# Nine homes for the V blocks, half of their loads begun by ScalarE, gates in groups of eight

## What is computed

```python
q = (xt @ w_q).reshape(T, PEER_HEADS, 2, PEER_DK_HALF)          # T = 512, D = 1024
s1, i1 = lax.top_k(s[:, :, 0], 16); s2, i2 = lax.top_k(s[:, :, 1], 16)
top_s, pos = lax.top_k(cand, 16)                                # 8 heads x 16 experts of 16384
gates = jax.nn.softmax(top_s, axis=-1)
a = jax.nn.gelu(jnp.einsum('cd,ced->ce', xc, u_table[ic]), approximate=False) * gc
out = jnp.einsum('ce,ced->cd', a, v_table[ic])
```

## Time and profile before

| | |
|---|---|
| median of 3 runs | 1637.96 us (1637.13 to 1638.74) |
| profiled execution, own time | 1638.74 us |
| its span | 1636.9 us, so 1.84 us lie around the span |
| TensorE | busy 1593.2 us, 97% |
| VectorE | busy 1275.3 us, 78% |
| ScalarE, GpSimd | 739.5 us, 929.4 us |
| DMA | 457.79 MB, mean 280 GB/s |
| stage V on TensorE | 1104.1 to 1622.3 us |

### The profile page before, as it was taken

How to read it: one execution, slowest core, us unless ns; L and a number is a source line. 1 busy time by engine, 2 the same in 40 slices (tenths; PEclk the granted TensorE clock), 3 DMA queues, 4 the chain that set the end, 5 groups by cost and what they waited for, 6 DMA issues and landing times.

```text
span 1636.9 us, 25955 instructions
## 1 busy us (share of the span) xinstructions
PE 1593.2 (97%) x9763; PEld 1484.6 (91%) x9763; DVE 1275.3 (78%) x2385; ACT 739.5 (45%) x1278; POOL 929.4 (57%) x558
## 2 busy tenths in 40 slices
PE   9999999999999999999999999997999999999996
PEld 7788777788888999999999999997999999999996
DVE  7876635654532899999999878757988899889894
ACT  5533335644321433346677788732333333333333
POOL 4545322434442898898766668786444555546530
PEclk9999999999999999999999999999999999999998
DMA  8321423365443899999988899999999999999981
GB/s 231 104 78 52 116 78 90 91 195 172 116 129 108 300 361 338 347 336 332 341 324 334 300 344 415 418 392 365 407 404 378 389 405 404 406 404 402 404 324 52
DMA packets 215828, 457.79 MB, mean 280 GB/s; under 512 B 14800, under 2 KB 106320, under 8 KB 214168
## 3 DMA queue, kind: packets, MB, share of 16 engines
q1 hardware_dynamic: 145304, 221.29, 39.8%
q0 software_dynamic: 46080, 167.79, 26.4%
q10 hardware_dynamic: 24320, 67.05, 10.6%
HBM read 401.59 MB, written 54.46 MB: 279 GB/s over the span
## 4 chain that ended last, share of the span: by engine, by line
PE 65%; DMA 14%; DVE 12%; issue 4%; ACT 2%; POOL 1%; SPq 0%; POOLq 0%; DVEq 0%; ACTq 0%
PE bank L294 17%; PE bank L296 17%; PE bank L295 17%; DMA raw<-in_v_tab 9%; PE bank L1999 5%; DMA rows<-in_v_tab,expert 2%; DMA mixbuf<-dense_gates 2%; PE x_rows L294 1%; PE x_rows L296 1%; PE x_rows L295 1%; ACT spl_a L284 1%; DVE rows L1376 1%; PE bank L906 1%; POOL spl_a L288 1%; DVE spl_a L288 1%
## 5 line engine op out<-in xcount | busy, mean ns | idle before, releaser
L288 POOL TENSOR_TENSOR spl_a<-raw,spl_a 128x1024 fp32r<-128x1024 f32 x170 | 411.4, 2422 | 217.8 <-ACT spl_a L284 216.1
L284 ACT ACTIVATE spl_a<-raw 128x1024 fp32r<-128x1024 f32 x294 | 309.8, 1056 | 419.1 <-PE bank L296 237.4
L1367 POOL DMA_INDIRECT rows<-in_v_tab,expert x160 | 252.9, 1580 | 216.8 <-DVE hot L1874 193.4
L294 PE MATMUL bank<-x_dense,spl_a 128*128 128x352 f32 x1024 | 335.7, 328 | 6.3 <-ACT gl L1588 6.0
L296 PE MATMUL bank<-x_dense,spl_a 128*128 128x352 f32 x1024 | 329.3, 322 | 0.0
L295 PE MATMUL bank<-x_dense,spl_a 128*128 128x352 f32 x1024 | 328.8, 321 | 0.0
L294 PE MATMUL bank<-aws,spl_a 128*128 128x352 f32 x768 | 249.6, 325 | 20.2 <-DVE aws L1854 17.9
L295 PE MATMUL bank<-aws,spl_a 128*128 128x352 f32 x768 | 248.2, 323 | 0.0
L296 PE MATMUL bank<-aws,spl_a 128*128 128x352 f32 x768 | 248.1, 323 | 0.0
L1376 DVE SCALAR_TENSOR_TENSOR rows<-rows,x_rows 128x1024 f32<-128x1024 f32 x154 | 186.0, 1211 | 28.1 <-DMA rows<-in_u_rows,expert 27.8
L1874 DVE SCALAR_TENSOR_TENSOR hot<-rows,dot_rows,hot 128x1024 f32<-128x1024 f32 x157 | 197.7, 1278 | 4.5 <-DMA rows<-in_v_tab,expert 4.5
(11 more groups left out here) (362 smaller groups left out, 3070.1 us busy)
## 6 DMA issues: line engine op xcount, KB each, us to landing
raw<-in_u_t SPq DMA_DIRECT2D x128, 512.0 KB, 6.2
raw<-in_v_tab SPq DMA_DIRECT2D x128, 512.0 KB, 9.7
dense_gates<-mixbuf ACTq DMA_DIRECT2D x11, 2048.0 KB, 10.9
raw<-in_w_in SPq DMA_DIRECT2D x42, 512.0 KB, 3.9
gelu_ux<-gl ACTq DMA_DIRECT2D x58, 352.0 KB, 6.2
mixbuf<-gelu_ux SPq DMA_DIRECT2D x19, 704.0 KB, 12.7
late_gates<-dense_gates ACTq DMA_DIRECT2D x4, 2816.0 KB, 37.3
mixbuf<-dense_gates ACTq DMA_DIRECT2D x3, 2816.0 KB, 36.5
```

What stands on the lines that cost most here:

```text
L284: eng.activation(spl(n, 0, slice(0, W)), raw[:, s, :], ACT.Copy).then_inc(hi_done, 1)
L288: eng.tensor_tensor(spl(n, 1, slice(0, W)), raw[:, n % RAW, :], spl(n, 0, slice(0, W)).bitcast(F32), ALU.subtract) \
L294: nc.tensor.matmul(out, w_hi, x_hi, start=first, stop=False)
L1367: pool.indirect_dma_start(out=rows[:, g % ROWS, :], out_offset=None, in_=u_rows[:, :] if g < STEPS else v_rows, in_offset=bass.IndirectOff ...
```

## The change

Four things are done.

1. **Raw homes.** The memory of `late_gates` becomes five more homes for raw V blocks (`raw_more`). V's blocks 7 to 11 go there as soon as stage U is over; from then on nine homes are used in turn, so that a load waits for the lower part of the block nine before and no longer four before. SyncE issues the loads of blocks 12, 14, 16, ... and ScalarE those of 13, 15, 17, ..., each at a step of V two apart.
2. **Gates.** They come in groups of 8 blocks (1408 KB, pieces of 1 KB) into two halves of `mixbuf`. Groups 0 and 1 come in stage U where the halves of group 0 came; group g comes at step 8g - 10 of V, and VectorE needs it at its step 8g - 2. All are issued by ScalarE, on the same queue as its V loads.
3. **Exponentials.** `EXP_AT` becomes 22, 46, 69, 93: the first two stand one step of U later.
4. **The start of V.** VectorE instead of GpSimd makes the lower parts of V's blocks 0 to 3, put between its last dot products, of which 6 and not 9 stand behind the wait for the gates, 4 and not 6 of them with the right operand in SBUF. The additions of the V rows are spread over 120 steps from step 2 on instead of 122 steps from step 0 on. The reading of GELU parts stands two steps later.

Its diff, without the lines that only move semaphores or rename:

```diff
@@ -108,7 +108,9 @@
 AWS = 4
 LAST = 2
 KEPT = 12
-GROUP = 16
+GROUP = 8
+MORE = 5
+FAR = 7
 VECTOR_LO = []
 WARM = 5
 
@@ -204,7 +206,8 @@
         x_space = ExitStack()
         x_dense = sb(x_space, "x_dense", [P, 2, KD, DT], F32R)
         x_space.close()
-        late_gates = sb(outer, "late_gates", [P, GROUP * DT])
+        late_space = sb(outer, "raw_more", [P, 2 * KD * DT])
+        raw_more = late_space[:, 0:MORE * W].rearrange("p (s c) -> p s c", s=MORE)
         tiles = sb(outer, "tiles", [P, 2, KD, P])
         dot_rows = sb(outer, "dot_rows", [P, 2 * KD * (T - DT - P)])
         z_row, g_row, a_row = [dot_rows[:, i * STEPS:(i + 1) * STEPS] for i in range(3)]
@@ -239,7 +245,7 @@
 
         def by_vector(n):
 
-            return n in VECTOR_LO or n >= V0 + LEAD
+            return n in VECTOR_LO or n >= V0
 
         def lo_count(n):
 
@@ -249,27 +255,51 @@
 
             eng.wait_ge(lo_vector if by_vector(n) else lo_done, lo_count(n))
 
+        def raw_home(n):
+
+            if n < V0 + FAR:
+                return n % RAW
+            at = (n - V0 - FAR) % (RAW + MORE)
+            return RAW + at if at < MORE else (V0 + FAR + at - MORE) % RAW
+
+        def raw_block(n):
+
+            s = raw_home(n)
+            return raw[:, s, :] if s < RAW else raw_more[:, s - RAW, :]
+
+        def raw_before(n):
+
+            return max([m for m in range(max(0, n - RAW - MORE), n) if raw_home(m) == raw_home(n)], default=None)
+
+        def block_loaded(n):
+
+            s = raw_home(n)
+            return unit_loaded[s] if s < RAW else more_loaded[s - RAW]
+
         def load_unit(sp, n):
 
-            if n >= RAW:
-                wait_lo(sp, n - RAW)
-            s = n % RAW
+            if raw_before(n) is not None:
+                wait_lo(sp, raw_before(n))
+            elif n >= RAW:
+                sp.wait_ge(unit_used, V0)
             if BR0 <= n < WO0:
                 c = (n - BR0) * P
-                dst = raw[:, s, :].rearrange("p (k c) -> p k c", k=KD)
+                dst = raw_block(n).rearrange("p (k c) -> p k c", k=KD)
                 sp.dma_start(dst[:, 0:4, :], w_a[:, c:c + P].rearrange("(k p) c -> p k c", p=P)) \
-                    .then_inc(unit_loaded[s], 16)
+                    .then_inc(block_loaded(n), 16)
                 sp.dma_start(dst[:, 4:8, :], w_b[:, c:c + P].rearrange("(k p) c -> p k c", p=P)) \
-                    .then_inc(unit_loaded[s], 16)
+                    .then_inc(block_loaded(n), 16)
             elif n < U0:
-                sp.dma_start(raw[:, s, :].rearrange("p (k c) -> p k c", k=KD), unit_source(n)) \
-                    .then_inc(unit_loaded[s], 16)
+                sp.dma_start(raw_block(n).rearrange("p (k c) -> p k c", k=KD), unit_source(n)) \
+                    .then_inc(block_loaded(n), 16)
             else:
-                sp.dma_start(raw[:, s, :], unit_source(n)).then_inc(unit_loaded[s], 16)
-
-        def loads_before(n, s):
-
-            return sum(2 if BR0 <= m < WO0 else 1 for m in range(s, n + 1, RAW))
+                sp.dma_start(raw_block(n), unit_source(n)).then_inc(block_loaded(n), 16)
+
+        def loads_before(n):
+
+            s = raw_home(n)
+            loads = sum(2 if BR0 <= m < WO0 else 1 for m in range(n + 1) if raw_home(m) == s)
+            return loads if s < RAW else loads + 1
 
         def last_step(n):
 
@@ -277,15 +307,14 @@
 
         def split_hi(eng, n):
 
-            s = n % RAW
-            eng.wait_ge(unit_loaded[s], 16 * loads_before(n, s))
+            eng.wait_ge(block_loaded(n), 16 * loads_before(n))
             if spl_before(n) is not None:
                 eng.wait_ge(unit_used, last_step(spl_before(n)) + 1)
-            eng.activation(spl(n, 0, slice(0, W)), raw[:, s, :], ACT.Copy).then_inc(hi_done, 1)
+            eng.activation(spl(n, 0, slice(0, W)), raw_block(n), ACT.Copy).then_inc(hi_done, 1)
 
         def split_lo(eng, n):
             eng.wait_ge(hi_done, n + 1)
-            eng.tensor_tensor(spl(n, 1, slice(0, W)), raw[:, n % RAW, :],
+            eng.tensor_tensor(spl(n, 1, slice(0, W)), raw_block(n),
                               spl(n, 0, slice(0, W)).bitcast(F32), ALU.subtract) \
                 .then_inc(lo_vector if by_vector(n) else lo_done, 1)
 
@@ -1311,9 +1338,9 @@
         first_half.close()
         mixbuf = sb(outer, "mixbuf", [P, 24 * DT])
         stage = mixbuf[:, 0:2 * NC * TB].rearrange("p (s c t) -> p s c t", s=2, c=NC)
-        gates_home = [mixbuf[:, 0:GROUP * DT], late_gates[:, :]]
+        gates_home = [mixbuf[:, i * GROUP * DT:(i + 1) * GROUP * DT] for i in range(2)]
         gl = sb(outer, "gl", [P, 4, DT])
-        gelu_home = [gl] + [mixbuf[:, (GROUP + 4 * i) * DT:(GROUP + 4 * i + 4) * DT].rearrange("p (c t) -> p c t", c=4)
+        gelu_home = [gl] + [mixbuf[:, (2 * GROUP + 4 * i) * DT:(2 * GROUP + 4 * i + 4) * DT].rearrange("p (c t) -> p c t", c=4)
                             for i in range(2)]
         rows = sb(outer, "rows", [P, ROWS, D])
         aws = sb(outer, "aws", [P, 2, AWS, DT], F32R)
@@ -1334,16 +1360,18 @@
         row_used = sem("row_used")
         z_gelu = sem("z_gelu")
 
-        def mix_gates(queue, group, first, count, mixed):
-
-            c = expert_chunk(GROUP * group + first)
+        def mix_gates(queue, group):
+
+            c = expert_chunk(GROUP * group)
             home = gates_home[group % 2].rearrange("p (b c t) -> p b c t", c=GROUP, t=TB)
-            tail = min(count, NC - c)
-            queue.dma_start(home[:, :, first:first + tail, :].rearrange("p b c t -> p b (c t)"),
-                            dense_d[:, :, c * TB:(c + tail) * TB].rearrange("b p x -> p b x")).then_inc(mixed, 16)
-            if tail < count:
-                queue.dma_start(home[:, :, first + tail:first + count, :].rearrange("p b c t -> p b (c t)"),
-                                dense_d[:, :, 0:(count - tail) * TB].rearrange("b p x -> p b x")).then_inc(mixed, 16)
+            tail = min(GROUP, NC - c)
+            queue.dma_start(home[:, :, 0:tail, :].rearrange("p b c t -> p b (c t)"),
+                            dense_d[:, :, c * TB:(c + tail) * TB].rearrange("b p x -> p b x")) \
+                .then_inc(gates_mixed[group % 2], 16)
+            if tail < GROUP:
+                queue.dma_start(home[:, :, tail:GROUP, :].rearrange("p b c t -> p b (c t)"),
+                                dense_d[:, :, 0:(GROUP - tail) * TB].rearrange("b p x -> p b x")) \
+                    .then_inc(gates_mixed[group % 2], 16)
 
         def mix_gelu(queue, part_no):
 
@@ -1434,7 +1462,7 @@
             LATE_STEPS = 15
             LATE_DOTS = 15
             SCORES_AT = [0, 0, 0, 8, 14, 19, 24, 30, 35, 41, 46, 52, 58, 64, 70, 76]
-            EXP_AT = [21, 45, 69, 93]
+            EXP_AT = [22, 46, 69, 93]
             SLOTS_AT = [None, 48, 72, 98]
             GATHER_AT = [4, 4, 4, 5, 6, 7, 7, 8, 9, 9, 10, 11, 11, 12, 13, 14, 14, 15, 17, 17, 18, 19, 20, 21, 22,
                          23, 24, 24, 25, 26, 27, 28, 29, 30, 30, 31, 32, 33, 34, 35, 36, 36, 37, 38, 39, 40, 41, 42, 42, 43, 44,
@@ -1445,7 +1473,7 @@
                          115, 115, 116, 117, 118, 119, 120, 121, 122, 123, 124, 124, 125]
             PAIR_DOTS = [0, 4, 8, 6, 7, 7, 7, 7, 7, 8, 6, 6, 6, 6, 6, 6]
             PAIR_QUADS = [0, 0, 0, 0, 0, 0, 0, 0, 0, 5, 5, 6, 7, 8, 8, 8]
-            LAST_DOTS = [3, 3, 3]
+            LAST_DOTS = [2, 2, 2]
             VECTOR_AT = []
             PIECES = 8
 
@@ -1470,15 +1498,17 @@
             f_wide, f_wide_last = sem("f_wide"), sem("f_wide_last")
             V_ORDER = [2, 3, 4, 5, 0, 1, 6, 7]
             AHEAD = 6
-            SBUF_DOTS = 6
+            SBUF_DOTS = 4
             turned = [[bank[0], bank[3]], [bank[1], bank[4]], [bank[2], bank[5]]]
             h_bank = [bank[4], bank[5]]
             SUM_SQ0, SUM_SQ1, BIAS, ROOT, INV = range(5)
-            ROW_STEPS = 122
+            ROW_STEPS = 120
+            ROWS_FROM = 2
 
             def value_steps(j):
 
-                return range(min(STEPS, j * STEPS // ROW_STEPS), min(STEPS, (j + 1) * STEPS // ROW_STEPS))
+                j -= ROWS_FROM
+                return range(min(STEPS, max(0, j) * STEPS // ROW_STEPS), min(STEPS, max(0, j + 1) * STEPS // ROW_STEPS))
 
 
             block = ctx.enter_context(nc.Block())
@@ -1512,13 +1542,18 @@
                             sp.dma_start(g_row[g * NX:(g + 1) * NX, SLOTS:STEPS],
                                          slot[0:NX, 1, 2, 2 * g:2 * g + 2, :].rearrange("p h k -> p (h k)")) \
                                 .then_inc(x_listed, 16)
-                    if U0 + LOAD_LEAD + j < N_UNITS:
+                    if j < NC:
                         load_unit(sp, U0 + LOAD_LEAD + j)
+                    elif j == NC:
+                        for n in range(V0 + LOAD_LEAD, V0 + LOAD_LEAD + MORE):
+                            load_unit(sp, n)
+                    elif j % 2 and V0 + LOAD_LEAD + MORE - 1 + j - NC < N_UNITS:
```

(32 more changed lines are left out.)

## The result

The changed kernel takes **1675.38 us** (median of 4 runs, 1673.10 to 1677.86), the kernel before 1638.35 beside it: ratio 1.0201 [1.0179, 1.0223], 2.0% slower. The prediction said 1634.2 and at most 1645. The profiled execution took 1676.11 us, its span is 1674.1. Stage V starts at 1104.0 us, as before (1104.1), and ends at 1659.6, not 1622.3: all of the 37 us are lost in V.

The account below looks back on a forecast made before the run. Matmuls and transfers were the candidate bounds of stage V, with transfers (404 GB/s against 415 asked) limiting the gain. Stage V -1.8 and exponentials -1.9 made -3.7 us, from 1637.96 to 1634.2 us; range 1622 to 1645.

Parts of the forecast that it names:

- Homes: Stage V's loads: issued about 12 blocks ahead, not 7; waits for V blocks go, and ScalarE's new waits cost nothing.
- The passage from U to V: Start of V: VectorE finishes about 7 us earlier, 1110 and not 1117, so weights are ready when TensorE wants them.
- The lower part of block 4: Sign at V's start: VectorE makes it at about 1110 us, with no 8 us wait of TensorE behind it.
- I take the 13.1 us as removed: Start of V: the 13.1 us TensorE loses there go, with 2 us left over.
- What the transfers allow: Stage V: TensorE asks for 415 GB/s against 404 available, so bytes set the sum: -9.5 + 5.5 + 2.2 = -1.8 us.
- The sum by bytes: V's start to block 116: 187.4 MB at 404 GB/s, not 396, take 463.8 us, 9.5 us less.
- The pieces of 1 KB: Gates of stage V: fourteen groups of 1.44 MB at 0.27 us per MB more cost 5.5 us, bounds nothing and 8.
- The dip of +2.2: Stage V: one dip as at 1230, a fifth below the rate for 10 us, left in at 2.2 us.
- gates come late: Rival, stage V: 1 KB pieces delay gates, deciding from 34 us of landing; 1650 us at 36.5; chance 0.13.
- Exponentials: First two exponentials one step later: first wait gone, second stays, -1.9 us, between 0 and -3.8.
- The end of the range at 0: Exponentials: the gain is nothing if transfers, full from 980 us on, eat it.
- The total: Whole kernel: -1.8 for stage V and -1.9 for the exponentials, -3.7 us, giving 1634.2 us.

Follow-up runs that it names:

- e1: Changed kernel with SyncE issuing all V loads, one at each step; 1640.93 us, ratio 0.9995 to the kernel before.
- e4: Changed kernel with gates from group 2 on read as 128 pieces of 11 KB from another place (output not right); 1628.62 us, ratio 0.9919.
- e7: Changed kernel with gates from group 2 on read as 512 pieces of 2816 bytes from another place (output not right); 1628.48 us, ratio 0.9907.
- e10: Changed kernel with gates from group 2 on read as 1024 pieces of 1408 bytes from another place (output not right); 1628.98 us, ratio 0.9922.
- e9: Kernel before with only the start of V changed (part 4 without the GELU steps); 1633.32 us, ratio 0.9954.
- e8: e1 (all V loads on SyncE) with the gates issued two steps earlier; 1631.97 us, ratio 0.9928 to the kernel before.
- e12: e8 with five homes for V blocks in place of nine; 1630.58 us, ratio 0.9932 to the kernel before.
- e5: Kernel before with only the first two exponentials one step later; 1642.22 us, ratio 0.9994.
- e6: Kernel before with the first two exponentials and the transposes of the second tile's slots one step later; 1640.13 us, ratio 0.9987.
- e3: Changed kernel with stage V's gates loads issued by SyncE, ScalarE still issuing every second V load; 1636.86 us, ratio 0.9962.
- e2: Changed kernel with ScalarE's V load issued ahead of the gates load in the same step; 1644.66 us, ratio 1.0015.

## Why the prediction was wrong

- **The step that failed:** "The issue of 57 loads is no work for ScalarE's datapath", under Homes, from which ScalarE's part was costed at nothing. I looked at whether the datapath was free (165 of 473 us busy) and not at how long its order is held. I named what is queued behind the new semaphore waits, and not behind the issue itself. In 14 places a V load stands directly behind 1408 pieces of gates; 12 hold the order for 80.7 us, and V ends 37 us later. Taking the loads off ScalarE (e1) or making the pieces fewer (e4, e7) removes all of it, and 1024 pieces (e10) leave at most 3.75 us at a time and none of the 37. In the kernel before nothing of V stood behind gates on that queue, so no row of it had the price. The one issue there directly behind 1408 pieces (of 512 bytes, the first part of a load of gates) took 0.66 us, at 1086.16, and gave no warning. The earlier trace rows bounded it from above all the same: an issue held until gates have landed would have been up to 26 us. No rival had this mechanism.
- **The passage from U to V** came as forecast in its parts: two weights in 1.68 us (1.8 forecast), dot products of 1.22, lower parts of 1.22. The lower part of block 4 came at 1112.5, not 1110: the dot products moved into the idle time waited for their rows (the last one 2.60 us, up to 1094.58), as the prediction had allowed, and the first lower part took 2.17. (The 0.88 us read as a weight in the earlier trace rows is a lower part of one, L1854; a weight undisturbed takes 0.88 as well, at 1104.66 in the changed kernel.) "I take the 13.1 us as removed": e9 measures 9.6 (V's blocks 4 to 12: 44.7 us before, 35.1 after).
- **What the transfers allow.** The sum by bytes held where it could be tested: -9.5 us forecast for V's start to block 116, -8.1 in e9 (465.4 against 473.5), at 403 GB/s. The pieces of 1 KB were put at +5.5; e8 takes 4.7 us more than e7 and 2.9 more than e4 (466.8, 462.1, 463.9), though who issues the loads, and how early the gates come, differs as well. The dip of +2.2 didn't come: in e8 no stretch of 10 us from 1110 to 1570 us is under 397 GB/s. But I had made the homes the means by which 404 GB/s is reached, and e9 and e12 reach 403 and 400 with four and five of them.
- **The rival "gates come late"** was there at a smaller size. I let it decide from 34 us of landing; in e1 they land in 30.9 (median) and VectorE waits 36.7 us, about 3 at each of 12 groups: eight steps of 30.6 us leave a load of 30.9 nothing. e8 shows its price: 0.9995 to 0.9928. The changed kernel itself shows one such wait, 2.5 us, ahead of the first hold; behind that none, presumably because the holds had slowed everything else, which no run tests.
- **Exponentials.** Forecast -1.9, measured nothing (e5). The room was read at the quads of step 54; the transposes of step 48 come first. The end of the range at 0, because transfers take it back, fits e6: V starts 1.6 us earlier and ends as before.
- **The total** of -3.7 us, a ratio of 0.9977, lies between e1 (0.9995, its interval holds it) and e8 (0.9928). That is luck and confirms nothing: it was made of terms of which the homes' part was credited to the wrong cause and the holds were missing.

What stays open: why two of 14 loads weren't held, where exactly the limit lies (behind 512 pieces hardly a hold, behind 1408 nearly always, with whatever else the queue still has), and how much of e8's gain over e9 (two chips, 0.26% apart, the intervals overlap) is real.

## What to carry to other kernels

Cost a DMA issue on a compute engine by what is already in that engine's DMA queue, in pieces and not in bytes, and by what stands behind it in program order. Put loads of many pieces on an engine that has nothing urgent behind them (in e3 the GELU parts were late even so), and not on one whose next instruction feeds TensorE; where that can't be, cut them into fewer, longer pieces. Long waits in the table of waits prove nothing until one sees that the engine at the end of the chain waits for them: 58.5 us went and gave nothing.

## What the runs showed of the hardware

- The issue of a 128-piece load directly behind 1408 pieces of 1 KB on the same queue took 4.93 to 9.45 us on ScalarE, in place of 0.33 to 0.35; 7 us later still 1.44 to 5.27 (e2); on SyncE's busier queue up to 19.30 (e3). Behind 1024 pieces it was 0.66 to 3.75 us, behind 512 0.62 to 1.37, behind 128 under 0.5.
- With SyncE's queue kept full by nine homes, its V loads were held 96 times, up to 5.28 us (e8); with five homes none took over 0.44 us (e12), and the kernel's time was the same.
- The same 1408 KB landed in 25.0, 17.7 and 10.7 us (medians) as 1024, 512 and 128 pieces, beside the same other traffic.
